# A hybrid two-layer trunk on one Trainium2 core: index key and head weights in one projected tile, and the first attention scores among the last key tiles

## The reference

```python
proj = h @ w_in                     # columns: q, k, v (1024 each), qi (8 heads of 64), ki (64), wi (8)
logits = einsum('bqhd,bsd->bqhs', qib, ki) * IDX_DIM ** -0.5
score = einsum('bqh,bqhs->bqs', wb, relu(logits))       # masked to admissible chunks of 64
_, idx = lax.top_k(score, 64)                            # the 64 keys that a query keeps
s_att = einsum('bqhd,bqkhd->bhqk', qb, kg) * HEAD_DIM ** -0.5 - slopes * dist
p = softmax(s_att);  out = einsum('bhqk,bqkhd->bqhd', p, vg)
x = x + g1 * (out @ w_out)
```

## Time and profile before

| | |
|---|---|
| median of 3 runs | 740.59 us (739.83 to 742.02) |
| the profiled execution | 741.73 us, its span 739.9 us |
| PE busy | 704.2 us, 95% of the span |
| DVE busy | 532.5 us, 72% |
| ACT busy | 414.3 us, 56% |
| POOL busy | 128.4 us, 17% |
| granted TensorE clock, mean | 0.993 of full speed |
| a 512 KB load for a dot, issued by POOL | median 4.6 us from issue to landing |

### The profile page before, as it was taken

The page is one execution under the profiler, slowest core; times in us unless marked ns, Lnnn a source line. Parts: engine busy times, 40 slices in busy tenths (PEclk is TensorE's granted clock), DMA queues, the critical chain, the costliest instruction groups (busy, mean ns, idle before and its releaser), DMA issues.

```text
span 739.9 us, 17363 instructions
## 1 busy us (share of the span) xinstructions
PE 704.2 (95%) x6920; PEld 642.7 (87%) x6920; DVE 532.5 (72%) x897; ACT 414.3 (56%) x681; POOL 128.4 (17%) x113
## 2 busy tenths in 40 slices
PE   3899999899999999999999999999999999999996
PEld 1578989569798999999998888889799999999994
DVE  4866778585678878778867876866487667666765
ACT  5355745565464656576567754354566555555553
POOL 1000101001035443444304175410000000000000
PEclk9899999999999999999999999999999999999999
DMA  8989978955756666555575045249435555555521
GB/s 308 396 320 401 363 264 284 330 211 217 286 180 208 247 228 229 176 170 182 185 279 175 31 165 181 89 140 395 150 114 177 185 185 193 171 175 191 174 83 58
DMA packets 46216, 157.14 MB, mean 212 GB/s; under 512 B 6048, under 2 KB 7344, under 8 KB 46160
## 3 DMA queue, kind: packets, MB, share of 16 engines
q1 hardware_dynamic: 41040, 139.87, 54.2%
q0 software_dynamic: 2960, 10.10, 3.9%
q10 hardware_dynamic: 2160, 6.38, 2.2%
HBM read 155.28 MB, written 1.05 MB: 211 GB/s over the span
## 4 chain that ended last, share of the span: by engine, by line
PE 87%; DVE 5%; issue 3%; ACT 2%; POOL 1%; DMA 1%; ACTq 0%; DVEq 0%; POOLq 0%
PE up L418 13%; PE up L420 13%; PE up L419 13%; PE acc L418 10%; PE acc L419 9%; PE acc L420 9%; PE gv L463 4%; PE acc L621 3%; DVE wlo L1234 2%; PE misc L522 1%; PE up L817 1%; PE up L804 1%; DMA ident<-in_ident 1%; PE acc L792 1%; DVE tmp L1264 1%
## 5 line engine op out<-in xcount | busy, mean ns | idle before, releaser
L1234 DVE TENSOR_TENSOR wlo<-raw,whi 128x1024 fp32r<-128x1024 f32 x188 | 252.2, 1356 | 56.9 <-ACT whi L873 52.2
L418 PE MATMUL up<-hh,whi 128*128 128x256 f32 x832 | 237.4, 285 | 2.3 <-DVE hl L1269 1.9
L420 PE MATMUL up<-hh,wlo 128*128 128x256 f32 x832 | 235.3, 283 | 0.0
L419 PE MATMUL up<-hl,whi 128*128 128x256 f32 x832 | 235.3, 283 | 0.0
L873 ACT ACTIVATE whi<-raw 128x1024 fp32r<-128x1024 f32 x185 | 192.5, 1052 | 43.8 <-PE acc L420 21.5
L418 PEld LDWEIGHTS up<-hh,whi 128*128 128x128 f32 x832 | 159.5, 192 | 8.9 <-issue 5.0
L419 PEld LDWEIGHTS up<-hl,whi 128*128 128x128 f32 x832 | 159.6, 192 | 0.0
L420 PEld LDWEIGHTS up<-hh,wlo 128*128 128x128 f32 x832 | 159.5, 192 | 0.0
L1552 DVE SCALAR_TENSOR_TENSOR ffn<-up,conv,ffn 128x254 f32<-128x254 f32 (+1 forms) x176 | 72.6, 474 | 44.4 <-ACT ffn L1081 44.0
L418 PE MATMUL acc<-ah,whi 128*128 128x256 f32 x352 | 99.8, 284 | 0.6 <-DVE wlo L1234 0.6
L419 PE MATMUL acc<-al,whi 128*128 128x256 f32 x352 | 99.6, 283 | 0.0
(11 more groups left out here) (266 smaller groups left out, 946.4 us busy)
## 6 DMA issues: line engine op xcount, KB each, us to landing
raw<-in_w SPq DMA_DIRECT2D x188, 512.0 KB, 3.7
mraw<-in_mw SPq DMA_DIRECT2D x32, 512.0 KB, 6.6
arena<-in_mw SPq DMA_DIRECT2D x32, 512.0 KB, 7.9
arena<-in_mw POOLq DMA_DIRECT2D x16, 512.0 KB, 4.6
raw<-in_w SPq DMA_DIRECT2D x12, 256.0 KB, 13.0
tmp<-in_mw ACTq DMA_DIRECT2D x4, 512.0 KB, 6.4
ffn<-in_mw ACTq DMA_DIRECT2D x4, 512.0 KB, 8.9
mraw<-in_mw ACTq DMA_DIRECT2D x4, 512.0 KB, 16.4
```

Source lines behind the costliest of these rows:

```text
L418: pe.matmul(out, w_h, xh, start=first, stop=False, skip_group_check=skip)
L419: pe.matmul(out, w_h, xl, start=False, stop=False, skip_group_check=skip)
L420: return pe.matmul(out, w_l, xh, start=False, stop=last, skip_group_check=skip)
L1234: dve.tensor_tensor(wlo[:, n % SPL, :], raw[:, n % RAW, :], whi[:, n % SPL, :].bitcast(F32), ALU.subtract).then_inc(lo_ready, 1)
```

## The change

1. **One tile less.** `ki` (64 columns), `wi` (8) and 56 columns of zeros share tile 0. The projection has 29 tiles, every later slot number falls by one (`q` is 5 to 12, `v` 13 to 20, `k` 21 to 28), and the first q tile joins the six that are projected by halves.
2. **The key's second copy.** ACT copies rows 0 to 63 of tile 0's bank to partitions 64 to 127 (`ki_odd`) just before it copies the tile itself; the index scores wait for that (`ki_ready`). The head weights are read from columns 64 to 71 of the transposed tile.
3. **Scores among the key tiles.** The order on PE becomes: tiles 21 to 26, `scores(0)`, `gemv(C_ATT)`, tile 27, `scores(1)`, tile 28, the wait for its copy, `gemv(C_ATT + 1)`, the pairs. ACT does `exps(0)` and `exps(1)` after it has copied tiles 27 and 28 out, DVE weaves its splits, dots, `tops` and `normed(0)` together, and the last round and the bias come one split earlier.
4. **The odd bias in bf16.** Since `hh` is still read by the key tiles, the odd bias goes into a new buffer `zb`, in bf16, with a bf16 identity. The row of zeros that opens PSUM banks lies in the same buffer, and DVE writes it after attention, no longer at the start.

```diff
-N_IN = 30
+N_IN = 29
-S_KI, S_WI, S_QI, S_Q, S_V, S_K = 0, 1, 2, 6, 14, 22
+S_KI, S_QI, S_Q, S_V, S_K = 0, 1, 5, 13, 21
...
+        zb = sb("zb", [P, 512], mybir.dt.bfloat16)
+        zrow, bias_e, ident_b = zb[0:1, :], zb[:, 0:384], zb[:, 384:512]
+        ki_odd = pt[HD:P, 0, :, :].rearrange("p e t -> p (e t)")[:, 512:512 + T]
...
         def scores(p, a):
...
-                    pe.matmul(bank, ident_r[:], bias_h[e], start=True, stop=False, skip_group_check=True)
                     if e == 0:
+                        pe.matmul(bank, ident_r[:], bias_h, start=True, stop=False, skip_group_check=True)
                         pe.matmul(bank, ident_r[:], bias_l, start=False, stop=False, skip_group_check=True)
+                    else:
+                        pe.matmul(bank, ident_b, bias_e, start=True, stop=False, skip_group_check=True)
...
-            gemv(C_ATT)
-            pe.wait_ge(bias_hi, 3)
-            pe.wait_ge(bias_lo, 1)
-            scores(0, 0)
-            scores(1, 1)
+            for n in range(S_K, N_IN):
+                pe.wait_ge(qkv_ready, n - KT - 1)
+                project(up[:, n % 2, 0:T], n)
+                if n == N_IN - 3:
+                    pe.wait_ge(vt_ready, 4)
+                    pe.wait_ge(bias_hi, 4)
+                    pe.wait_ge(bias_lo, 1)
+                    scores(0, 0)
+                    gemv(C_ATT)
+                elif n == N_IN - 2:
+                    scores(1, 1)
+            pe.wait_ge(qkv_ready, N_IN - KT)
             gemv(C_ATT + 1)
...
             for n in range(RAW):
                 act.wait_ge(slot_used, n + 1)
+                if n == S_KI:
+                    act.activation(ki_odd, idx_bank[n][0:HD, :], ACT.Copy).then_inc(ki_ready, 1)
...
+                if n == N_IN - 5:
+                    act.activation(ident_r[:], ident[:], ACT.Copy).then_inc(bias_hi, 1)
+                    act.activation(ident_b, ident[:], ACT.Copy).then_inc(bias_hi, 1)
+                    act.wait_ge(bias_ready, 2)
+                    act.activation(bias_h, bias[:, 0, :], ACT.Copy).then_inc(bias_hi, 1)
+                    act.activation(bias_e, bias[:, 1, :], ACT.Copy).then_inc(bias_hi, 1)
+                    act.activation(idle[:], epsc[:], ACT.Exp)
+                elif n >= N_IN - 2:
+                    exps(n - N_IN + 2, n - N_IN + 2)
...
+            split_lo(26)
+            dot(4)
+            split_lo(27)
+            dve.wait_ge(bias_hi, 3)
+            dve.tensor_tensor(bias_l, bias[:, 0, :], bias_h.bitcast(F32), ALU.subtract).then_inc(bias_lo, 1)
+            dot(5)
+            split_lo(28)
+            dot(6)
+            split_lo(29)
             tops(0, 0)
+            split_lo(30)
+            dot(7)
             tops(1, 1)
+            normed(0, 0)
             split_lo(N_IN + SPL - 1)
-            normed(0, 0)
...
+            dve.memset(zrow, 0.0).then_inc(set_up, 1)
...
-    w_first = np.concatenate([ki, ki, wi, np.zeros((D, P - IH), f), w_in[:, qi0:ki0], w_in[:, 0:D]], axis=1)
+    w_first = np.concatenate([ki, wi, np.zeros((D, HD - IH), f), w_in[:, qi0:ki0], w_in[:, 0:D]], axis=1)
```

More of the change, by code:

```diff
@@ L345, in _ @@
                     load_w(n, i)
-            for n in range(W_OUT, W_OUT + RAW):
+            for n in range(W_OUT + 1, W_OUT + RAW):
                 load_w(n)
@@ L480, in open_bank @@
             def open_bank(bank):
-                pe.matmul(bank, zrow[:, 0:P], zrow[:], start=True, stop=True, skip_group_check=True)
+                pe.matmul(bank, zrow[:, 0:P], zrow, start=True, stop=True, skip_group_check=True)
             def part(out, n, tiles, phase):
@@ L555, in half @@
                 mm.then_inc((first_used, slot_used)[h], 1)
-            pe.wait_ge(set_up, 5)
+            pe.wait_ge(set_up, 4)
             pe.wait_ge(ones_in, 16 * N_ONES)
@@ L584, in score @@
                     mm = pe.matmul(acc[:, h % 4, (h // 4) * T:(h // 4) * T + keys],
-                                   qkv[r:r + HD, S_QI + h // 2, qt * P:(qt + 1) * P], qkv[r:r + HD, S_KI, 0:keys],
+                                   qkv[r:r + HD, S_QI + h // 2, qt * P:(qt + 1) * P],
+                                   ki_odd[:, 0:keys] if h % 2 else qkv[0:HD, S_KI, 0:keys],
                                    start=True, stop=True)
@@ L596, in _ @@
             for qt in range(2):
-                mm = pe.transpose(misc[:, qt * P:(qt + 1) * P], qkv[:, S_WI, qt * P:(qt + 1) * P], ident[:])
+                mm = pe.transpose(misc[:, qt * P:(qt + 1) * P], qkv[:, S_KI, qt * P:(qt + 1) * P], ident[:])
             mm.then_inc(idx_done, 1)
+            pe.wait_ge(ki_ready, 1)
             score(0, 1, T)
@@ L624, in _ @@
                 mm.then_inc(slot_used, 1)
[L625 to L629, removed]
             def scores(p, a):
@@ L692, in _ @@
                 project(acc[:, m % 4, 0:T], W_OUT + m)
+            pe.wait_ge(set_up, 5)
             norm(1, C_OUT // 2, misc[:, T:2 * T], open_rest, open_first, lambda: gemv(C_OUT))
@@ L1005, in _ @@
                     act.activation(crow, crow, ACT.Silu).then_inc(crow_ready, 1)
[L1006 to L1014, removed]
             def exps(p, a):
@@ L1036, in turned_out @@
                                ACT.Copy).then_inc(act_hi, 1)
-            act.activation(bias_h[1], bias[:, 1, :], ACT.Copy).then_inc(bias_hi, 1)
-            act.activation(idle[:], epsc[:], ACT.Exp)
-            exps(0, 0)
-            exps(1, 1)
+            for n in range(S_K, N_IN):
+                tile_out(n)
+                if n < S_K + 4:
+                    act.activation(vt[:, (n - S_K) // 2, ((n - S_K) % 2) * 512:((n - S_K) % 2) * 512 + 512], acc[:, n - S_K, :],
+                                   ACT.Copy).then_inc(vt_ready, 1)
+                if n == N_IN - 5:
[7 more added lines that the diff above has]
+                    exps(n - N_IN + 2, n - N_IN + 2)
             row_out(C_ATT // 2)
@@ L1287, in _ @@
             dve.memset(misc[:], 0.0).then_inc(set_up, 1)
-            dve.memset(zrow[:], 0.0).then_inc(set_up, 1)
             dve.memset(cond[:, :, 0], 0.0).then_inc(set_up, 1)
@@ L1468, in _ @@
             for n in range(4, 16):
-                split_lo(n + 11)
+                if n < 15:
+                    split_lo(n + 11)
                 top_round(n)
@@ L1479, in _ @@
                 dve.scalar_tensor_tensor(bias[:, e, :], ndist, slope[:, e:e + 1], msk, ALU.mult, ALU.add).then_inc(bias_ready, 1)
-            for n in range(27, 31):
-                split_lo(n)
-                dot(n - 23)
-            dve.wait_ge(bias_hi, 2)
-            dve.tensor_tensor(bias_l, bias[:, 0, :], bias_h[0].bitcast(F32), ALU.subtract).then_inc(bias_lo, 1)
-            split_lo(31)
             def tops(p, a):
```

7 lines of the change are left out of this document (3 added, 4 removed).

## The result

The changed kernel took 734.17 us in the median of its four runs (733.92 to 737.0), the kernel before 740.29 in four runs beside it (739.83 to 742.02): ratio 0.9915, interval 0.9887 to 0.9943. Its profiled execution was the slowest of the four: 737.0 us, span 735.0, mean granted clock 0.990. The sum for a profiled execution had been 737.01.

The account below looks back on a forecast made before the run. TensorE bounds the projection's stream (busy 65.37 of 65.48 us), and later idles waiting for normalising. Saving 2.88 for the tile and 1.84 for the idle, 4.72 together, takes 740.59 to 735.9 us; range 734.3 to 738.0.

Parts of the forecast that it names:

- The sum: Over the stretch through attention, 13.26 replaces 17.98 us on TensorE: 4.72 less, so 737.01 for a profiled execution.
- Part 1, the tile: In the projection's stream, one tile less saves 2.88 us on TensorE; nothing moves before the stream.
- Part 2, the key's copy: After the first half-tiles, one more ScalarE copy of at most 0.39 us is hidden and costs nothing.
- Part 3, the order: Between the last key tiles, earlier scores fill TensorE's idle of 1.84 us before the first transposes.
- The rooms: Slack before TensorE needs other engines' work: 0.8 split, 0.9 bias, 4 for tile 25's copy, 0.7 normalising, in us.
- Part 4, bf16: In the scores, eight odd-bias products in bf16 change nothing; bounds 0.8 us lost to 0.76 gained.
- the 735.1: The time if the odd bias gained 0.76 us from faster bf16 weight loads, by the skill's rule taken alone.
- From the profile to the median: For the whole kernel, 4.72 taken from the median of 740.59 gives 735.9; about 0.3% (2.2 us) counted as no change.
- The likeliest case: In attention, tile and idle are both won and no new wait appears: 735.9 us, chance 0.70.
- The slower rival: Before the first scores, a late bias stops TensorE 7.5 us: 743.4; loss from 4.72 late; chance 0.05.

Follow-up runs that it names:

- e2: The kernel before with one tile less and the key's second copy, old order of the scores; 737.7 us, ratio 0.9955.
- e1: The changed kernel again without an edit, with its own profile; 733.88 us, ratio 0.9912.
- e4: The kernel before again without an edit, with a second profile; 741.33 us, ratio 1.0001.
- e5: The changed kernel with one unused tile of zeros behind the weights in HBM; 736.03 us, ratio 0.9946.
- e8: The changed kernel with the rest of the even bias written behind two more splits and two dots on VectorE; 741.94 us, ratio 1.0018.
- e9: The changed kernel with 24 more matmuls and one ScalarE copy at the very end; 735.39 us, ratio 0.9925.
- e16: The changed kernel with one more VectorE subtraction behind its last operation, repeated on another chip; 735.12 us, ratio 0.9931.
- e13: The changed kernel with one more 512 KB load by SyncE and its wait behind the output; 740.29 us, one execution.
- e14: The changed kernel with one more VectorE subtraction of a tile behind its last operation; 737.95 us, one execution.
- e3: The kernel before with all 30 tiles but the new order of scores, the bf16 odd bias and the late zero row; 739.76 us, ratio 0.9979.
- e15: The changed kernel a further time without an edit, as control on the same chip; 735.87 us, ratio 0.9928.
- e12: The changed kernel a further time without an edit, beside the form with TensorE's later wait; 736.36 us, ratio 0.9926.

## Why the prediction was right and where it failed

- *Part 1, the tile.* 2.88 forecast, 2.87 measured (e2). Right from the stream on. The first step that failed is its opening sentence, "The first six tiles stay six, so nothing moves before the stream": the time ahead of the stream was put at nothing for a reason that does not cover it. An unchanged order does not make an unchanged start. Everything up to the index transposes hangs on the first reduction, which waits for the identity's landing, and that came at 11.04 in the profile before and at 9.54 in the changed kernel's. Over all profiles but the two on the chip with no 30-tile profile, the first reduction stands at 10.84 on average in five with 30 tiles and at 9.53 in eleven with 29; the index transposes at 57.75 and 56.26. So the profiles put this term at 1.3 to 1.5 us. The timed executions give it less: with each program's own stretch from index to norm taken off, the medians of those with 29 and with 30 tiles are still 1.3, 0.9 and 0.3 us apart on the three chips (e1 to e4, e5 to e8, e9 to e16 without e13 and e14). That there is such a term is shown; its size and its cause stay open.
- It did not show at once in the two profiles that I had to compare, since the changed kernel's had a stretch at the lower clock at 43 to 47 us and reached the index transposes at 57.96 against 57.99. In the spans, 739.9 - 735.0 = 4.9 is 4.70 from the index transposes to the norm behind attention, 0.03 before them and 0.20 in the state-space mixer.
- *Part 2, the key's copy.* Nothing, as forecast. In the changed kernel ScalarE makes it at 45.35, and behind the next copy it stands idle for TensorE, so the 0.38 had room:

```profile
45.35 0.38 ACT L974 ACTIVATE arena<-acc 64x256 f32<-64x256 f32 x1
47.42 0.38 ACT L975 ACTIVATE arena<-acc 128x256 f32<-128x256 f32 x1 [1.29 <-PE acc L556]
```

- *Part 3, the order.* 1.84 forecast, 1.88 measured (e3). The rooms were sized right. Split of tile 26 done at about 116.6 (115.44 + 1.15), I had 116.7; rest of the bias done by 119.33, I had 119.5; copy of tile 25 at 119.25, I had 119.5; normalising of pair 0 done at 132.94, I had 132.9, 0.60 before TensorE comes. None decided, and neither a wait on the bias nor one on normalising came back in the changed kernel.
- *Part 4, bf16.* Nothing, as forecast: from the bf16 product to the next start 120.97 - 120.71 = 0.26; in the kernel before, the odd bias in fp32r had 132.25 - 131.99 = 0.26 too. (The 0.18 that the prediction read is the distance behind the rest of the even bias, not behind the product that changes.) All eight products agree, with 0.26 to 0.27 in either kernel. The weights load in 96 ns instead of 188, as the Trainium skill, "TensorE: Matmul & The Clock Gate", section "Weight-path perf modes", would have it, but the load was not what TensorE waited for; so the reason behind the 735.1 is refuted, though that figure lay nearer to the first median. Pair 0's scores take 1.48 instead of 1.58, which is not the bf16 product: the first bias product has its successor after 0.18 behind a key tile (120.53 - 120.35), where behind a chunk or other scores it had 0.28.
- *The sum.* 4.72 forecast; 4.68 to 4.73 measured for the stretch in the eight profiles of the table that keep the change's order. The forecast of 737.01 for a profiled execution met one of 737.0, but by luck: the earlier start that I had left out and a stretch at the lower clock cancelled.
- *From the profile to the median.* Here the second step failed: I subtracted 4.72 from one median of three executions and took 0.3% as all that executions do by themselves. The first four of the changed kernel held three of the quicker group and gave 734.17; nineteen gave 735.87, and 82 of the kernel before 741.1, not 740.59. The 1.7 us between the forecast of 735.9 and the first 734.17 are the draw of those four (735.87 - 734.17). So the gain is about 5.2, of which 4.7 was forecast. That nineteen lie so near to the forecast of 735.9 is luck too: a base that was 0.5 too low stood against 0.5 of gain that I had left out. The low end of my range, 734.3, allowed for unknown costs in attention and for nothing that the rest of the program does by itself; with a start that moves by 1.3 and two groups 2.5 us apart (734.11 to 736.58) it should have reached to about 733.
- *Chances.* The likeliest case was the one that happened in attention. The slower rival was far: e8 delays the bias by 5.4 us (1.02 of room and 4.37 of wait) to end 1.39 behind the kernel before.

## What to carry to other kernels

Price a change by the stretch that it touches, between two events that every version has, and repeat the profile: such a stretch repeated within 0.05 us here while whole executions moved by 4. Before a median of three or four runs is trusted to 0.3%, ask for the clock of each run and compare like with like. A wait put on TensorE costs its length and, where the granted clock falls behind it, the time that the work then takes longer at the lower level: 4.4 us became 6.1.

## What was not expected of the hardware

- A single idle of 4.21 us brought TensorE's granted clock down to a mean of 0.66 over the next 5 us; it was still 1.00 during the idle and for the first us of work behind it.
- Far shorter idles can be followed by the lower clock too, in one execution and not in another of the same program: 1.84 us (e15 and not e12), 1.00 us (the first profile and not e1).
- The 64 KB identity, issued at 3.04 us by POOL in every program, landed 6.2 to 8.2 us later, and it is what TensorE's first matmul waited for.
- The first activation behind the exponential's table load starts 0.01 us after the end of the load's 1.28 us (117.85, 119.14).
